# First attention: eight heads one by one, and the same heads in four pairs on the two halves of the TensorE array

## What is computed

```python
def stick_breaking_attention(q, k, v):
    for blk in range(S // SB_BLOCK):            # 2 blocks of 128 queries
        ...
        z = jnp.einsum('bthd,bshd->bhts', qb, kb).astype(jnp.float32) * scale
        log_not = jnp.where(strict, jax.nn.log_sigmoid(-z), 0.0)
        suffix = lax.cumsum(log_not, axis=3, reverse=True) - log_not
        a = jnp.where(strict, jnp.exp(jax.nn.log_sigmoid(z) + suffix), 0.0).astype(v.dtype)
        outs.append(jnp.einsum('bhts,bshd->bthd', a, vb))
...
proj = h @ w_in[l]
q, k, v, p_in, gm_u, gm_v, gate_in = jnp.split(proj, IN_SPLITS, axis=-1)
gates = jax.nn.sigmoid(gate_in.reshape(B, S, N_BRANCH, D))   # 3 x 1024 columns of proj
```

## Time and profile before

| | us |
|---|---|
| median of 3 runs | 1027.43 (1025.7 to 1028.62) |
| the profiled execution | 1026.62, of which 1024.8 is the span of the trace |
| PE busy | 1010.8 (99%) |
| DVE, ACT, POOL busy | 719.6, 492.0, 108.4 |
| from the first gate unit to the small products after unit 9 | 66.28 to 144.51 |

### The profile page before, as it was taken

How to read it: one execution, slowest core, us unless ns; L and a number is a source line. 1 busy time by engine, 2 the same in 40 slices (tenths; PEclk the granted TensorE clock), 3 DMA queues, 4 the chain that set the end, 5 groups by cost and what they waited for, 6 DMA issues and landing times.

```text
span 1024.8 us, 16248 instructions
## 1 busy us (share of the span) xinstructions
PE 1010.8 (99%) x6616; PEld 886.9 (87%) x6616; DVE 719.6 (70%) x882; ACT 492.0 (48%) x559; POOL 108.4 (11%) x83
## 2 busy tenths in 40 slices
PE   8999999999999999999999999999999999999998
PEld 8997778899999888986899999988886689999997
DVE  6869657987667787854887767677976776445664
ACT  6455564553444436432554343445556665343431
POOL 1031000000010000225001000010001301000000
PEclk9999999999999999999999999999999999999999
DMA  9984345749788784595639877786461536665641
GB/s 319 368 277 155 129 136 182 286 168 343 258 285 282 277 274 146 170 311 156 224 110 346 284 281 276 254 284 222 171 226 56 171 118 212 199 198 175 201 165 42
DMA packets 120031, 223.77 MB, mean 218 GB/s; under 512 B 6622, under 2 KB 21408, under 8 KB 119968
## 3 DMA queue, kind: packets, MB, share of 16 engines
q1 hardware_dynamic: 117584, 214.97, 61.6%
q0 software_dynamic: 2256, 7.88, 2.4%
q10 hardware_dynamic: 128, 0.03, 0.0%
HBM read 217.17 MB, written 1.05 MB: 213 GB/s over the span
## 4 chain that ended last, share of the span: by engine, by line
PE 88%; DVE 7%; issue 2%; ACT 1%; DMA 1%; POOL 1%; SPq 0%; DVEq 0%; ACTq 0%; POOLq 0%
PE ps L461 84%; DMA ada_raw<-in_ada_w 1%; PE ps L1120 1%; DVE lo L367 1%; PE ps L951 1%; ACT aS L1977 1%; DVE X L922 1%; PE ps L817 1%; POOL aS L2422 1%; DVE stat L2322 1%; PE ps L1510 0%; DMA X<-in_x 0%; DVE y_tmp L921 0%; ACT hi L356 0%; PE ps L1717 0%
## 5 line engine op out<-in xcount | busy, mean ns | idle before, releaser
L367 DVE TENSOR_TENSOR lo<-raw,hi 128x2048 fp32r<-128x2048 f32 x151 | 349.2, 2319 | 221.1 <-ACT hi L356 220.7
L356 ACT ACTIVATE hi<-raw 128x2048 fp32r<-128x2048 f32 x151 | 289.1, 1915 | 303.2 <-PE ps L461 274.8
L461 PE MATMUL ps<-hTh,hi 128*128 128x256 f32 x992 | 265.7, 286 | 1.1 <-DVE lo L367 0.6
L461 PE MATMUL ps<-hTh,lo 128*128 128x256 f32 x992 | 262.4, 283 | 0.0
L461 PE MATMUL ps<-hTl,hi 128*128 128x256 f32 x992 | 261.0, 283 | 0.0
L461 PEld LDWEIGHTS ps<-hTh,hi 128*128 128x128 f32 x992 | 182.1, 192 | 4.0 <-issue 2.8
L461 PEld LDWEIGHTS ps<-hTl,hi 128*128 128x128 f32 x992 | 181.7, 192 | 1.5 <-issue 1.2
L461 PEld LDWEIGHTS ps<-hTh,lo 128*128 128x128 f32 x992 | 182.2, 192 | 0.0
L461 PE MATMUL ps<-hi,hidh 128*128 128x512 f32 (+1 forms) x424 | 164.6, 388 | 0.0
L461 PE MATMUL ps<-hi,hidl 128*128 128x512 f32 (+1 forms) x424 | 163.5, 386 | 0.0
L461 PE MATMUL ps<-lo,hidh 128*128 128x512 f32 (+1 forms) x424 | 163.4, 385 | 0.0
(11 more groups left out here) (248 smaller groups left out, 857.8 us busy)
## 6 DMA issues: line engine op xcount, KB each, us to landing
raw<-in_mlp_w SPq DMA_DIRECT2D x64, 1024.0 KB, 5.2
ada_raw<-in_ada_w SPq DMA_DIRECT2D x44, 1024.0 KB, 7.5
raw<-in_w_in SPq DMA_DIRECT2D x20, 1024.0 KB, 7.7
raw<-in_w_ff_in SPq DMA_DIRECT2D x16, 1024.0 KB, 5.4
raw<-in_w_ff_out SPq DMA_DIRECT2D x16, 1024.0 KB, 5.3
raw<-in_attn_w_qkv SPq DMA_DIRECT2D x12, 1024.0 KB, 6.1
raw<-in_conv_w_in SPq DMA_DIRECT2D x8, 1024.0 KB, 6.7
taps<-u_pad SPq DMA_DIRECT2D x64, 71.0 KB, 5.5
```

Of the source, the lines that this page charges most:

```text
L356: nc.scalar.activation(hi[:, slot], raw[:, slot], ACT.Copy).then_inc(hi_made, 1)
L367: nc.vector.tensor_tensor(lo[:, slot], raw[:, slot], hi[:, slot].bitcast(F32), ALU.subtract).then_inc(lo_made, 1)
L461: return nc.tensor.matmul(o, lhs, rhs, start=start, stop=False, skip_group_check=True)
```

## The change

The loop's order changes on PE, ACT and DVE. Scores of heads 2k and 2k+1 are issued together after the even unit s = 2k, first both large matmuls and then both small ones; so are their values, after unit s = 2k+2. The suffix sum of the even head 2k comes after unit 2k+1, and that of the odd head 2k+1 between the two halves of unit 2k+2 (the new hook `middle` of `unit_x`). ACT runs two `softplus` in a row, and takes the exponential of the odd head ahead of the even step's `hi`; DVE runs the odd head's argument ahead of the even step's `lo`, and two `log_not` in a row behind it. No arithmetic, tile or bank is added. The diff, whole but for its header and a few lines around it:

```diff
...
-        def unit_x(pe, u, j, act_h, act_l, k0, outs, first, nk=4, cols=512, final=False, need=None, tail=None):
+        def unit_x(pe, u, j, act_h, act_l, k0, outs, first, nk=4, cols=512, final=False, need=None, tail=None,
+                   middle=lambda: None):
...
             for tt in range(TT):
+                if tt:
+                    middle()
                 for c in range(parts):
...
-            def scores(h):
-                if h == 0:
+            def both(k):
+                return [(2 * k + i, slice(HD * i, HD * i + HD)) for i in range(2)]
+            def scores(k):
+                if k == 0:
                     pe.wait_ge(qkv_kept, 2)
-                if h >= 2:
-                    pe.wait_ge(arg_done, h - 1)
-                r = slice(HD * (h % 2), HD * (h % 2) + HD)
-                k = h // 2
-                nc.tensor.matmul(ps[:, 4 + h % 2, 0:SEQ], kT[r, k, 0:P], qT[r, k, :], start=True,
-                                 stop=False, skip_group_check=True)
-                nc.tensor.matmul(ps[:, 4 + h % 2, SEQ:384], kT[r, k, P:SEQ], qT[r, k, P:SEQ],
-                                 start=False, stop=False, skip_group_check=True).then_inc(z_done, 1)
+                else:
+                    pe.wait_ge(arg_done, 2 * k)
+                for h, r in both(k):
+                    nc.tensor.matmul(ps[:, 4 + h % 2, 0:SEQ], kT[r, k, 0:P], qT[r, k, :], start=True,
+                                     stop=False, skip_group_check=True)
+                for h, r in both(k):
+                    nc.tensor.matmul(ps[:, 4 + h % 2, SEQ:384], kT[r, k, P:SEQ], qT[r, k, P:SEQ],
+                                     start=False, stop=False, skip_group_check=True).then_inc(z_done, 1)
...
-            def values(h):
-                pe.wait_ge(a_done, h + 1)
-                if h >= 2 and h % 2 == 0:
-                    pe.wait_ge(o_lo, h // 2)
-                a = sbt[:, h % 2, 2]
-                r, at = slice(HD * (h % 2), HD * (h % 2) + HD), (h // 2 % 2) * SEQ
-                v = slice(h * HD, h * HD + HD)
-                mm(pe, ps[r, 7, at:at + SEQ], vS[:, 0, v], a[:, 0:SEQ], True)
-                mm(pe, ps[r, 7, at + P:at + SEQ], vS[:, 1, v], a[:, SEQ:384]).then_inc(av_done, 1)
+            def values(k):
+                pe.wait_ge(a_done, 2 * k + 2)
+                if k:
+                    pe.wait_ge(o_lo, k)
+                at = (k % 2) * SEQ
+                for h, r in both(k):
+                    mm(pe, ps[r, 7, at:at + SEQ], vS[:, 0, h * HD:h * HD + HD], sbt[:, h % 2, 2, 0:SEQ], True)
+                for h, r in both(k):
+                    mm(pe, ps[r, 7, at + P:at + SEQ], vS[:, 1, h * HD:h * HD + HD],
+                       sbt[:, h % 2, 2, SEQ:384]).then_inc(av_done, 1)
...
                     pe.wait_ge(gate_kept, g - 1)
+                odd_head = s % 2 == 0 and 2 <= s <= SB_HEADS
                 unit_x(pe, U_GATE + s, None, hTh, hTl, 4 * (s % 2), lambda tt, c: ps[:, bank + tt],
-                       s % 2 == 0)
-                if s < SB_HEADS:
-                    scores(s)
-                if 1 <= s < SB_HEADS + 1:
+                       s % 2 == 0, middle=(lambda: suffix(s - 1)) if odd_head else lambda: None)
+                if s % 2 and s < SB_HEADS:
                     suffix(s - 1)
-                if 2 <= s < SB_HEADS + 2:
-                    values(s - 2)
+                if odd_head:
+                    values(s // 2 - 1)
+                if s % 2 == 0 and s < SB_HEADS:
+                    scores(s // 2)
                 if s == 9:
...
+            def weights(h):
+                act.wait_ge(arg_done, h + 1)
+                a = sbt[:, h % 2, 2]
+                nc.scalar.activation(a, a, ACT.Exp).then_inc(a_done, 1)
             def o_split(k, bank, cols):
...
                     gate_from_bank(5, ACT.Sigmoid)
+                if s % 2 == 0 and 2 <= s <= SB_HEADS:
+                    weights(s - 1)
                 act_step(act, U_GATE + s)
-                if s < SB_HEADS:
+                if s % 2 == 0 and s < SB_HEADS:
                     softplus(s)
-                if 1 <= s < SB_HEADS + 1:
-                    h = s - 1
-                    act.wait_ge(arg_done, h + 1)
-                    a = sbt[:, h % 2, 2]
-                    nc.scalar.activation(a, a, ACT.Exp).then_inc(a_done, 1)
-                if s % 2 and s >= 3 and s < SB_HEADS + 2:
-                    k = (s - 3) // 2
+                    softplus(s + 1)
+                if s % 2 == 0 and 2 <= s <= SB_HEADS:
+                    k = s // 2 - 1
                     act.wait_ge(av_done, 2 * k + 2)
                     o_split(k, 7, slice((k % 2) * SEQ, (k % 2 + 1) * SEQ))
+                if s % 2 and s < SB_HEADS:
+                    weights(s - 1)
                 if s == 9:
...
+            def argument(h):
+                dve.wait_ge(sfx_done, h + 1)
+                t3 = sbt[:, h % 2, 2]
+                nc.vector.tensor_tensor(t3, t3, ps[:, 6, 0:384], ALU.add).then_inc(arg_done, 1)
             for s in range(12):
+                if s % 2 == 0 and 2 <= s <= SB_HEADS:
+                    argument(s - 1)
                 dve_step(dve, U_GATE + s)
-                if 1 <= s < SB_HEADS + 1:
-                    h = s - 1
-                    dve.wait_ge(sfx_done, h + 1)
-                    t3 = sbt[:, h % 2, 2]
-                    nc.vector.tensor_tensor(t3, t3, ps[:, 6, 0:384], ALU.add).then_inc(arg_done, 1)
-                if s < SB_HEADS:
+                if s % 2 and s < SB_HEADS:
+                    argument(s - 1)
+                if s % 2 == 0 and s < SB_HEADS:
                     log_not(s)
+                    log_not(s + 1)
                 if s == 1:
                     gating_norm()
-                if s % 2 and s >= 3 and s < SB_HEADS + 2:
-                    k = (s - 3) // 2
+                if s % 2 == 0 and 2 <= s <= SB_HEADS:
+                    k = s // 2 - 1
                     dve.wait_ge(o_hi, k + 1)
...
                                             hidh[:, k].bitcast(F32), ALU.subtract).then_inc(o_lo, 1)
```

## The result

The changed kernel takes **1032.26 us** (median of 6 executions, 1031.13 to 1034.69) beside 1027.93 us (6 executions, 1025.67 to 1028.65) for the kernel before. The ratio is 1.0051, 95% interval 1.0039 to 1.0063: the change costs 0.5%. The forecast was 1031.8 us, in a range of 1028.5 to 1034.8.

What follows compares the result with a forecast made beforehand. PE bounds the kernel, but a loop through DVE makes it wait: 7.6 us less work and 12.0 us of waits lengthen the stage by 4.4 us. 1026.62 plus 4.4 is 1031.0, with 0.8 for the median 1031.8 us; range 1028.5 to 1034.8.

Steps and rivals of the forecast that it cites:

- The removed work: PE in the gate stage: two heads' scores or values in the time of one, 7.6 us less PE work.
- The loop: From one odd suffix sum to the next, through PE, ACT and DVE: 16.98 us, against 14.84 us for PE alone.
- The waits: PE idle in the gate stage, for DVE's arguments and one ACT exponential: 12.0 us in all.
- list of signs: Expected in the changed profile: five L2110 waits, one over 3 us, an exponential wait near 1.7 us, turns of 16.9 to 17.0.
- Moved instructions: Behind the stage and in SP's loads: the shift is carried on; SP's later load costs nothing, 2.8 us if uncovered.
- Rival 1: Paired heads on PE don't overlap, pairs cost 1.68 and 1.58 us: +7.7 us, 1035.1 us; chance 0.08.
- Rival 2: PE's waits for the even head's argument do not close, all 12.0 us go: 7.6 us gained, 1019.8 us; chance 0.06.
- Rival 3: TensorE's clock falls to 1.2 GHz in the 3.3 us wait before suffix 1: +2.0 us more, 1033.8 us; chance 0.08.

Runs made afterwards that it cites:

- first profile: Profile of the changed kernel, no further edit, in its first set of runs; the profiled execution took 1032.27 us.
- the extra instruction: One more 128x384 DVE instruction behind each `log_not` of heads 2 to 7: 1035.09 us in the changed kernel, 1027.47 us in the kernel before.
- both edits: Changed kernel with the even head's argument ahead of `lo` in odd steps and `gating_norm` moved from step 1 to step 8: 1020.42 us, ratio 0.9937.
- second profile: Profile from running the changed kernel again with no further edit: 1033.29 us, ratio 1.0047.
- four sets: The kernel before, unedited, in the four sets where it ran beside the clock experiments' kernels: 31 of 81 executions with a fall.
- first wait filled: Changed kernel with twelve 128x128 filler matmuls on PE ahead of suffix sum 1, nothing else: 1029.41 us, ratio 1.0025.

## Why the prediction was right

**The removed work.** Forecast: pairs in 0.81 and 0.86 us, from the second attention. Measured: 0.81 and 0.85 us. That the heads alternate here and follow one another there made no difference.

**The loop.** Forecast 16.98 us, measured 16.89, the same in both turns. Term by term in the profile after, from the suffix sum at 104.57 on and, for DVE's part, in the turn before it: suffix sum 0.87 (forecast 0.90), `lo` 2.21 and 2.20 (2.21 twice), two `log_not` 5.61 (5.60), `hidl` 0.34 (0.42; the forecast took its length and not the step to the next instruction), argument to PE 0.69 (0.60).

**The waits.** Forecast 0.78, 3.30, 1.73, 1.88 and twice 2.14. Measured 0.72, 3.16, none in the first profile and 1.58 in the second, 2.03 (1.79 in the second), 2.05 and 2.04. The prediction's list of signs has five waits for L2110; its own sum has four, and four came. Counted from the first scores, the first values were forecast at 19.84 us and came at 19.84, suffix sum 7 at 66.70 and came at 66.68, the small products at 76.95 and came at 76.91. The experiment with the argument ahead of `lo` shows the cause of the repeated waits, the one with the extra instruction that the loop runs through DVE, the one with both edits that the sum of PE's work was right.

**Moved instructions.** Cost forecast at nothing; from 148.57 to 364.36 the changed kernel takes 215.79 us, the kernel before from 144.51 to 360.39 takes 215.88 us.

**Rival 1**, no overlap, falls with the pairs' lengths. **Rival 2**, waits that don't close, was not this kernel; with two DVE edits it is. It was priced at 1019.8 us and the version with both edits takes 1020.4 and 1020.1 us. The condition given there was too small for that price: with the even heads' argument early and nothing else, the wait for head 1's exponential stays (3.81 us) and the time is 1026.91 us; the norm of the gate has to move too.

**Rival 3**, the clock, is where the argument fell short though the total holds. The fall came true, in the first profile behind the very wait that was named, and the Trainium skill ("TensorE: Matmul & The Clock Gate", the section on HAM oscillation) was right to warn that TensorE's clock goes down again when the engine pauses for long. The pauses in the example that the Trainium skill gives in that section last about 3 to 5 us; here falls stand behind waits of 2.04 and 0.93 us too, and the measurement decides. Three things were wrong in the prediction. The price: put at 2.0 us there, it was 0.2 us. The half clock lasted 3.4 us and ended before the values, which waited for the exponential anyway; the prediction let all 3.73 us of work behind the wait run at half clock and hid too little of it. The condition: it was taken for a question of this one long wait, and the second profile shows that wait without a fall and a fall behind a wait of 2.04 us, where it costs 1.6 us. In the MLP tail the falls stand behind waits of 0.93 to 1.21 us with four one-column matmuls behind them, in five profiles; in five others waits of 0.64 to 0.97 us at the same place bring none. And the base: the kernel before falls too, in some four of ten executions, at the MLP tail, at a price of some 2 us (median 1026.5 us with a full clock, 1028.7 with one fall, in the four sets). One profiled execution with a full clock did not show it; the spread of the times given, 1025.7 to 1028.6 us, could have, and the prediction added the difference between median and profiled execution, 0.8 us, without asking what it was.

So the 1031.8 us came out near 1032.26 us for a reason that is only partly the forecast's. The stage's 4.38 us (76.95 less 72.57) was right to 0.04 us, with some luck: without the half clock the stage takes 76.69 us, 4.12 us more than before. On top come falls that cost in the changed kernel, and falls that cost in the kernel before. In the medians of the first comparison they nearly cancel (4.33 us; the mean clocks of the kernel before are not known for that set, but three of its six times are 1028.4 us or more, where full-clock executions end at 1027.5 in the later sets), in the later set they don't quite (1033.29 against 1027.85, 5.4 us).

**What stays open.** Whether a fall at the MLP tail is more likely because of what happened 300 us earlier. The changed kernel with its first wait filled had a full clock in 10 of 12 executions, its profile without the wait at the tail; the counts suggest a link but no run separates them, because the wait at the tail depends on when the load of `ada_raw` lands. DVE waits for it 2.61 and 2.31 us in the two profiles of the changed kernel and 1.29 us in the one with the first wait filled, and no run shows why. It is open too what, beside the length of a wait, decides whether the clock falls behind it.

## What to carry to other kernels

A pairing that halves small matmuls on PE is worth only what the producer of its inputs can follow: add up the loop from one use of a shared bank to the next through all engines, and put what PE waits for ahead of what nobody waits for yet. Here the same change costs 4.3 us with DVE's argument behind `lo` and gains 6.5 to 7.8 us with two groups of DVE instructions moved. Where PE waits a microsecond or more in the middle of dense work, look at the granted clock in stretches of a few microseconds and at the mean clock of every execution: a fall costs up to 1.6 us here, shows in no row of the page, and explains much of the spread between executions.

## What the hardware showed that was not expected

- TensorE's clock fell behind waits from 0.93 us (MLP tail) to 3.81 us and stayed full behind one of 3.15 us; it was at half for some 3.4 us each time, in the gate stage and in the MLP tail alike.
- A fall that is followed by a wait costs next to nothing: filling the wait ahead of it gave 0.2 us in that place (stage 76.69 against 76.91 us). Where PE is the path it costs 1.4 to 1.6 us.
- Two heads on two halves of the array take the time of one, for 64-row and for 64-column matmuls in plain float32: 0.85 against 0.84 us and 0.81 against 0.79 us.
- DVE's `tensor_scalar` on 128x384 elements from and to SBUF takes 0.36 us, against 0.55 us for the one that reads PSUM in the same timeline.
